# The order of the query tiles in a differential attention stage

## The reference

```python
def diff_attention(q, k, v, bias_table, lam_p, subln_g, lam_init):
    ...
    def block(args):                       # one block of 128 queries, all keys
        ...
        allowed = (kpos[None, :] // CHUNK) <= (qpos[:, None] // CHUNK)     # CHUNK = 64
        s = jnp.einsum('bhmqd,bhmkd->bhmqk', qi, k, ...) * ATTN_SCALE + bias
        p = jax.nn.softmax(jnp.where(allowed, s, -jnp.inf), axis=-1)
        attn = p[:, :, 0] - lam * p[:, :, 1]
        return jnp.einsum('bhqk,bhkd->bhqd', attn.astype(v.dtype), v)
    ...
    o = rms_norm(o, subln_g) * (1.0 - lam_init)
```

## Time and profile before

| | us |
|---|---|
| median of 3 runs | 2934.63 (2934.42 to 2936.46) |
| the profiled execution | 2935.31 |
| its span (first to last instruction) | 2933.6 |
| PE busy | 2656.7 (91%) |
| DVE busy | 1154.5 (39%) |
| ACT busy | 1019.0 (35%) |
| the 64 steps of diff_attn, from the trace | 665.2 to 1067.9 |

### The profile page before, as it was taken

One profiled execution on the slowest core, in us unless ns is written; L12 is line 12 of the kernel. 1 busy time (PEld: TensorE's weight loads), 2 busy tenths in 40 slices (PEclk: granted clock), 3 DMA queues, 4 the chain that ended last, 5 costly groups with the idle time before them and its releaser, 6 DMA issues. The chain is left out here.

```text
span 2933.6 us, 44852 instructions
## 1 busy us (share of the span) xinstructions
PE 2656.7 (91%) x16292; PEld 2252.2 (77%) x16292; DVE 1154.5 (39%) x2983; ACT 1019.0 (35%) x2516; POOL 307.9 (10%) x193
## 2 busy tenths in 40 slices
PE   3999999988888876679969999999996999999898
PEld 2788888986677655558858888888995888888687
DVE  5411111108889865445531111111101555555465
ACT  3211111006777754432221111111001777777221
POOL 1121212100000002110011122122100000100100
PEclk9999999999999998889979999999997999999899
DMA  4433322129414028866563433322216677875552
GB/s 140 128 123 107 122 79 82 50 68 182 101 29 74 1 89 188 184 184 225 190 204 108 129 123 114 101 79 70 68 47 154 127 155 156 165 145 123 183 202 85
DMA packets 235396, 358.27 MB, mean 122 GB/s; under 512 B 63464, under 2 KB 132756, under 8 KB 234692
## 3 DMA queue, kind: packets, MB, share of 16 engines
q1 hardware_dynamic: 225140, 316.95, 41.0%
q0 software_dynamic: 10064, 38.80, 4.5%
HBM read 222.45 MB, written 133.21 MB: 121 GB/s over the span
## 5 line engine op out<-in xcount | busy, mean ns | idle before, releaser
L509 PE MATMUL p_acc<-p_h_hi,p_w_hi 128*128 128x512 f32 x1440 | 566.5, 393 | 16.1 <-DVE p_h_lo L457 16.1
L509 PE MATMUL p_acc<-p_h_lo,p_w_hi 128*128 128x512 f32 x1440 | 563.2, 391 | 0.0
L509 PE MATMUL p_acc<-p_h_hi,p_w_lo 128*128 128x512 f32 x1440 | 563.0, 391 | 0.0
L509 PEld LDWEIGHTS p_acc<-p_h_hi,p_w_hi 128*128 128x128 f32 x1440 | 272.0, 189 | 74.6 <-DVE p_h_lo L457 19.4
L509 PEld LDWEIGHTS p_acc<-p_h_hi,p_w_lo 128*128 128x128 f32 x1440 | 271.7, 189 | 56.8
L509 PEld LDWEIGHTS p_acc<-p_h_lo,p_w_hi 128*128 128x128 f32 x1440 | 272.0, 189 | 55.3
L1034 DVE CUSTOM_DVE_ANT_0 c_logits<-c_logits,c_bias 128x640 f32<-128x640 f32 (+4 forms) x256 | 191.5, 748 | 228.7 <-PE c_logits L961 220.7
L305 DVE SCALAR_TENSOR_TENSOR p_lo_out<-p_acc,p_hi_out 128x512 fp32r<-128x512 f32 x116 | 80.2, 691 | 498.3 <-ACT p_hi_out L289 498.3
L289 ACT ACTIVATE p_hi_out<-p_acc 128x512 fp32r<-128x512 f32 x116 | 69.4, 598 | 513.6 <-PE p_acc L509 513.5
L506 PE MATMUL p_acc<-p_w_hi,p_h_lo 128*128 128x256 f32 (+1 forms) x768 | 224.3, 292 | 0.0
L506 PE MATMUL p_acc<-p_w_lo,p_h_hi 128*128 128x256 f32 (+1 forms) x768 | 224.3, 292 | 0.0
(11 more groups left out here) (161 smaller groups left out, 4036.3 us busy)
## 6 DMA issues: line engine op xcount, KB each, us to landing
scr_qh<-p_hi_out SPq DMA_DIRECT2D x116, 256.0 KB, 2.5
scr_ql<-p_lo_out SPq DMA_DIRECT2D x116, 256.0 KB, 2.9
scr_gt<-p_f_out SPq DMA_DIRECT2D x128, 128.0 KB, 1.9
p_w_raw<-in_w_in_odd POOLq DMA_DIRECT2D x16, 1024.0 KB, 6.7
c_q<-scr_qh SPq DMA_DIRECT2D x64, 256.0 KB, 8.0
c_q<-scr_ql SPq DMA_DIRECT2D x64, 256.0 KB, 9.8
o_o<-scr_ot SPq DMA_DIRECT2D x6, 2048.0 KB, 9.2
o_g<-scr_gt SPq DMA_DIRECT2D x6, 2048.0 KB, 15.0
```

Of the source, the lines that this page charges most:

```text
L509: last = nc.tensor.matmul(acc[v % 4][:, :], wt[:, half, c * n + cc * P:c * n + (cc + 1) * P], ht[:, c, b * BLK:(b + 1) * BLK], **flags)
```

## The change

The steps of a head are taken from both ends: heads 1 to 3 in the order 15, 0, 14, 1, 13, 2, 12, 3, 11, 4, 10, 5, 9, 6, 8, 7. Head 0 keeps tiles 0 to 3 first and then takes 15, 4, 14, 5, 13, 6, 12, 7, 11, 8, 10, 9. A step now waits for every block of its head up to its own that no step before has waited for. `out` and the sums of squares are indexed by head and tile in place of the step, so that the norm and the stores behind the steps stay as they were. Instructions are neither added nor removed; each tile's own are the same.

```diff
-        steps = [(h, i) for h in range(A_HEADS) for i in range(TILES)]
+        def mixed(first, last):
+            tiles = range(first, last)
+            return [i for pair in zip(reversed(tiles), tiles) for i in pair][:len(tiles)]
+
+        steps = [(h, i) for h in range(A_HEADS) for i in (list(range(TPB)) + mixed(TPB, TILES) if h == 0 else mixed(0, TILES))]
...
-                if m == 0 and k == 0 and i % TPB == 0:
-                    pe.wait_ge(head_loaded[h % 2][i // TPB], 16 * LOADS * (h // 2 + 1))
+                if m == 0 and k == 0:
+                    for n in needs[g]:
+                        pe.wait_ge(head_loaded[h % 2][n], 16 * LOADS * (h // 2 + 1))
...
-                nc.vector.tensor_scalar(out[:, g, :], o_ps[:, :], inv_sum[:, g % 4, 0:1], None, ALU.mult).then_inc(out_done, 1)
+                h, i = steps[g]
+                nc.vector.tensor_scalar(out[:, h * TILES + i, :], o_ps[:, :], inv_sum[:, g % 4, 0:1], None, ALU.mult).then_inc(out_done, 1)
```

More of the change, by code:

```diff
@@ L556, in diff_attn @@
         LOADS = 13
-        steps = [(h, i) for h in range(A_HEADS) for i in range(TILES)]
+        def mixed(first, last):
+            tiles = range(first, last)
+            return [i for pair in zip(reversed(tiles), tiles) for i in pair][:len(tiles)]
+        steps = [(h, i) for h in range(A_HEADS) for i in (list(range(TPB)) + mixed(TPB, TILES) if h == 0 else mixed(0, TILES))]
+        needs, arrived = {}, 0
+        for g, (h, i) in enumerate(steps):
+            arrived = 0 if g % TILES == 0 else arrived
+            needs[g] = range(arrived, max(arrived, i // TPB + 1))
+            arrived = max(arrived, i // TPB + 1)
         parts = {}
@@ L777, in squares @@
                     act.wait_ge(sq_done, g)
-                nc.scalar.activation(square[:, :], out[:, g, :], ACT.Square, accum_out=ssq[:, g:g + 1]).then_inc(sq_done, 1)
+                h, i = steps[g]
+                at = h * TILES + i
+                nc.scalar.activation(square[:, :], out[:, at, :], ACT.Square, accum_out=ssq[:, at:at + 1]).then_inc(sq_done, 1)
             for g in range(G + 3):
```

## The result

| | before | after |
|---|---|---|
| median of 4 runs, us | 2935.55 (2934.42 to 2936.89) | 2993.88 (2991.66 to 2995.50) |
| span of the profiled execution | 2933.6 | 2992.2 |
| the 64 steps of diff_attn, first QK to last PV | 402.3 | 462.6 |
| all that stands behind them | 1866.1 | 1866.1 |
| a head (from D of tile 15 to D of the next head's tile 15; the first such stretch) | 99.9 | 112.1 |

What follows compares the result with a forecast made beforehand. The prediction took a chain round the engines, with no engine always busy, to bound the 64 steps: 2935.3 + 47 (longer turns and head 0's loads) + 23 (PE's clock) = 3005 us, range 2970 to 3033.

Steps and rivals of the forecast that it cites:

- The bound: In diff_attn's 64 steps, no engine always busy; a chain going round the engines sets the time.
- Mixing fills the gaps: Rival for the 64 steps: small tiles' work fills large tiles' waits, 90 us a head, 2911 us; chance 0.05.
- only the loads cost: Rival: turns cost as the two steps did apart, only head 0's 17 us load wait is added, 2952; chance 0.05.
- A turn of 15.9, 15.1, 14.4, 13.5, 12.6, 11.9, 11.7, 13.6: Times in us of a head's eight large-and-small pairs, 108.7 together against 99.9 before.
- the ring: Five banks where a large tile wants eight; forecast to hold QK1 no longer than PV, 5.7 us after QK0 starts.
- The load wait: Head 0's fifth step, tile 15, waits for blocks 1 to 3: PE starts at 692, 17 us of standstill.
- Head 0 as reckoned through: Head 0 from 692 by its turns to M1 of tile 15 of head 1, put at 790.1.
- The clock, +23: PE's clock falls in turns of tiles 15 to 12: 12 falls of 1.6 us, four of 1 us in head 0.
- The sum: Steps end at 1115.1 without the clock, near 1138 with it; kernel 3005 us.
- the clock holds: Rival: PE's clock stays up, so only longer turns and loads cost, 2982 us (2972 to 2990); chance 0.22.
- E1 ahead of D: Turn from tile 15 to 14: 2.8 us of E1 until D starts, plus 0.2 from M1, 3.0 in all.

Runs made afterwards that it cites:

- heads123: Kernel before with heads 1 to 3 alternating large and small tiles, head 0 in rising order; 2974.04 us, ratio 1.0122.
- warm: Changed kernel plus 16 unused identity transposes on PE ahead of T of tiles 12 to 15 in heads 1 to 3; 2976.16 us, ratio 1.0141 to before.
- late_mix: Changed kernel with head 0 taking tiles 0 to 7 rising, then 15, 8, 14, 9, 13, 10, 12, 11; 2978.18 us, ratio 1.0140 to before.
- two_by_two: Kernel before with heads 1 to 3 in the order 15, 14, 0, 1, 13, 12, 2, 3, ..., head 0 rising; 2944.25 us, ratio 1.0030.

## Why the prediction was right

The forecast was 3005 us and a slower kernel with a chance of 0.92; measured were 2993.9, 11 less and inside the range. Step by step:

- **The bound, and that the small tile doesn't fill the gaps:** right. DVE's busy time for a head didn't change, its idle time did. *Mixing fills the gaps* (2911) and *only the loads cost* (2952) are out by far; heads123 alone costs 38.6 us without any wait for loads. The Trainium skill (Perfetto Trace Analysis, Optimization Strategy) says that interleaving regimes may help; in this kernel it lost 2%, in a stage whose regimes do differ.
- **A turn of 15.9, 15.1, 14.4, 13.5, 12.6, 11.9, 11.7, 13.6:** warm has them without the clock: 15.5, 14.8, 14.3, 13.2, 12.2, 11.6, 11.3, 14.4 from D to D. Seven of eight are 0.1 to 0.4 too long in the forecast, and the last, from tile 8 to the next head's tile 15, is 0.8 too short. The sum is 107.2 for a head in place of 108.7. (108.7 - 99.9 is 8.8 and not 8.9; the forecast's sum doesn't use it.) In the first turn the 0.4 lies in QK0 and PV, which the forecast took by their durations: from start to start they take 1.83 and 3.49 us in place of 2.0 and 3.7. The chain and its pieces were the ones named: in the turn above, 2.38 us of idle ahead of D (2.8 + 0.2 from M1 to D forecast, 3.0 measured: 791.32 less 788.33), PV 3.74, and 1.65 ahead of M1. What the forecast didn't see is how little of PV's 3.7 can be had back, since the ring takes over 1.4 us further on.
- **The load wait:** 17.60 us, forecast 17; PE starts the fifth step at 691.50, forecast 692. late_mix, without it and with two pairs fewer, is 17 us shorter.
- **Head 0 as reckoned through:** D of tile 15 of head 1 at 791.32 in after, forecast M1 at 790.1 and 3.0 more, 793.1. The 1.8 us fall on the restart and the first M (1.0: D of tile 15 at 703.27, forecast 704.3), the five turns to tile 10 (0.3: 15.45, 14.89, 14.64, 13.48 and 13.85 are 72.3, forecast 72.6) and the last two (0.5).
- **The clock, +23:** the mechanism was right and its size a little high, 17.7 by warm. In heads 1 to 3 it fell 10 times where 12 were forecast, at 1.8 us each in place of 1.6. The two that are missing belong to the turn from tile 15: the forecast had PE idle for 3 us ahead of T there, with a short PV before it. But this PV is that of the last tile of the head before (tile 9 or 7, 2.47 or 2.02 us), and the idle time is only 1.32 us in head 1 and 1.76 in heads 2 and 3. In the turns of head 0 the clock didn't fall at all, 1.00 in the window above, where four falls were forecast at 1 us. There the partner is a middle tile, and PE's gaps stayed under 1.6 us; that this kept the clock up is my reading.
- **The sum:** the steps end at 1126.5, forecast 1115.1 + 23 = 1138.1. Of these 11.6 us, 5.8 are there at D of tile 15 of head 1 (4 for the clock in head 0, and the 1.8 above), 3.7 come in heads 1 and 2 (112.1 + 114.4 in place of 2 x (108.7 + 6.4)), and 2.1 in head 3.
- **The rival that came next,** *the clock holds* (2982): warm is this case but for its added transposes, and gave 2976. In the changed kernel the clock fell, as the earlier trace rows let expect. No large errors cancelled in the sum: too short were only the last turn of a head (0.8), the load wait (0.6) and the price of a fall (0.2).

So of the +58, 20 are head 0 (most of it the standstill for loads), 17.7 the clock in heads 1 to 3, and 21, the rest of the 38.6, the longer chain there. Left open are the price of E1 ahead of D by itself, which wasn't tried, why the clock fell at T of tile 15 in head 2 and not in head 3, and which of the two differences makes the pairs of two_by_two cheap. No kernel that does the whole of the work was faster than the kernel before.

## What to carry to other kernels

In this kernel, where the engines work in order and wait for each other in a circle, work of different size side by side didn't even out: a small step couldn't get past what stood ahead of it, and a large one found nothing to cover it. Look for the same where the queues are like these. Before reordering, follow one turn of the chain in the timeline at a place where such neighbours already stand, and add it up; here that one place, with a few rows for the sizes, gave the time of seven turns in eight within 0.4 us at full clock. And where a change opens gaps on PE, or takes work from it, look at its clock before judging the change by its time.

## What the hardware did that was not expected

- In the new order, less work for PE hardly made the kernel faster: with most of PV cut, the clock was low for 145 us in place of 92, and the time was +56 us in place of +58. With 192 useless transposes added to the whole work it was 17.7 us shorter.
- Gaps of nearly the same length didn't have the same result. Before, PE's gap of 2.47 us at 73.09 was followed by a low clock. In after, the same place has 2.40 us and the clock holds (timeline; then the window):

```profile
73.47 0.50 PE L509 MATMUL p_acc<-p_h_hi,p_w_hi 128*128 128x512 f32 x1 [2.40 <-DVE p_h_lo L457]
...
73.00:76.00 3.00, 2.53 (x15) 2.19 (x16) 2.83 (x8) 1.53 (x3) 0.00 (x0) 1.00 0.47 175
```

  Before had two such falls there, after none, in code that the change doesn't touch. Ahead of this place after was 0.4 us the later of the two, and from 158 us on it was 2.3 us the earlier; 1.6 us of that are left where the stage starts. In the same way a gap of 1.76 us at the start of head 2, ahead of T of tile 15, was followed by a low clock (0.50 from 906.0 to 909.3 us) and the same gap a head later was not (timeline of after):

```profile
904.87 2.37 PE L655 MATMUL a_turned<-keep_ident,a_prob 128*128 128x128 f32 x11 [1.76 <-DVE a_prob L735]
...
1019.27 1.32 PE L655 MATMUL a_turned<-keep_ident,a_prob 128*128 128x128 f32 x8 [1.76 <-DVE a_prob L735]
```

  So the length of a gap alone doesn't tell whether the clock falls, and some us of a comparison can come from this and not from the edit.
